# Gathering expert rows of u and v in turn, instead of four and four

## The chip, the cores and the metric

The kernel runs on one core of one Trainium2 chip. The metric is the device time of one execution in microseconds (us); the kernel before has a median of 3765.66 us over three runs, from 3763.17 to 3771.36 us.

## The reference, cut to what matters

The model is one layer of a decoder: attention with a latent cache beside a short convolution, and then a channel mixer (PEER) that looks up experts. It is computed for 1024 prompt rows and 8 sample rows, all in float32. The part that the change touches is the mixer:

```python
def peer_block(x, w_query, sub_keys, expert_u, expert_v):
    ...
    experts = jnp.take_along_axis(cidx, pos, axis=-1)      # 8 heads x 16 picks = 128 per row
    g = jax.nn.softmax(top_s, axis=-1)
    u = expert_u[experts]
    v = expert_v[experts]
    a = jax.nn.gelu(jnp.einsum('td,thkd->thk', x, u).astype(jnp.float32), approximate=False)
    return jnp.einsum('thk,thkd->td', (g * a).astype(x.dtype), v)
```

So each of the 1024 rows picks 128 experts. Of each it needs one row of u (1024 floats) for a dot product, and one row of v (1024 floats), which is added to the result with a weight made from that dot product.

## The kernel before, in words

The prompt is cut into 8 tiles of 128 rows. A tile has two halves of work. The front (`stages_of`, L80) is everything up to the choice of the experts: norm, projections, four attention heads, output projection, eight query projections with their top-16 searches, and `select`. The other half is the experts' part. The loops of all engines run it for tile `it` beside the front of tile `it + 1`; beside the eighth tile runs the front of the sample rows, which reads pages of the cache.

The experts' part of a tile has 128 slots. A slot is one gather of u and one of v, each 128 partitions by 1024 floats, 524,288 bytes. Slots go in groups of G = 4, so a tile has 32 groups, g = 0 to 31 (the trace's L numbers are lines of the kernel before). `u_ring` and `v_ring` hold RING = 8 slots each, two groups.

What each engine does for group g of a tile, in the order of its own queue:

- DVE (L1339 and on): the four dot products of group g + 1 (`dot_group`, L1301; each waits for its own u gather), then the weights of group g (`weigh_group`, L1307), then its part of the front stages that `beside(g, T)` puts there, about one stage a group.
- ACT: the gelu of group g + 1 (L918, waits for all four dot products), then four diagonal matrices of group g from its weights (L925), then its front stages.
- PE: its part of the front stages, then `v_group` of group g (L676): 16 matrix products of `v_ring` with the diagonals, in two pairs of slots. A pair's two slots of `v_ring` are told free with the last products of the pair.
- POOL: it only issues gathers (L1438), all from one queue and in order. It waits for `u_free` of a slot (the dot product made 8 slots earlier) or `v_free` (the matrix products made 8 slots earlier), then issues. At the start of a tile it waits for the picks.
- SP: it loads the weights of the front in pieces of 1 MB, from its own DMA queue.

The order of POOL's queue is written out by hand in `tile` (L1454) and `gather_group` (L1441). There the loop over g is:

```python
for g in range(GROUPS):
    if g + 1 < GROUPS:
        gather_group(it, g + 1, "expert_u", u_ring, u_loaded)
    gather_group(it, g, "expert_v", v_ring, v_loaded)
```

Of the kernel before, what the change touches and what calls it, by code (L numbers as in the profile page):

```python
# [45 lines left out]
SLOTS = PH * TOPK  # L46
# [17 lines left out]
G = 4  # L64
GROUPS = SLOTS // G
RING = 2 * G
# [63 lines left out]
def build(nc, a, out):  # L130

    with ExitStack() as ctx:
        def sb(name, shape, dt=F32):
            return ctx.enter_context(nc.sbuf_tensor(name, shape, dt))

        on = namedtuple("Events", EVENTS)(*[ctx.enter_context(nc.semaphore(n)) for n in EVENTS])
        w_loaded = [ctx.enter_context(nc.semaphore(f"w_loaded{r}")) for r in range(WR)]
        u_loaded = [ctx.enter_context(nc.semaphore(f"u_loaded{r}")) for r in range(RING)]
        v_loaded = [ctx.enter_context(nc.semaphore(f"v_loaded{r}")) for r in range(RING)]
# [24 lines left out]
        u_ring = sb("u_ring", [P, RING, D])  # L164
        v_ring = sb("v_ring", [P, RING, D])
        ident2 = sb("ident2", [P, HB])
        diag = sb("diag", [P, RING, HB])
        pick_cur = sb("pick_cur", [P, SLOTS], U32)
# [90 lines left out]
        def waited(eng):  # L259


            eng.nop(nofuse=True)
# [1168 lines left out]
        @block.gpsimd  # L1431
        def _(pool):
            pool.memset(ckv_rows[:], 0.0).then_inc(on.zeroed, 1)
            pool.memset(ckvT[:], 0.0).then_inc(on.zeroed, 1)
            pool.memset(krT[:], 0.0).then_inc(on.zeroed, 1)

            def gather(table, ring, slot, loaded, pick):
                pool.indirect_dma_start(ring[:, slot, :], None, a[table][0],  # L1438
                                        bass.IndirectOffsetOnAxis(ap=pick, axis=0)).then_inc(loaded[slot], 16)

            def gather_group(it, g, table, ring, loaded):  # L1441
                if g * G == SLOTS // 2:

                    pool.wait_ge(on.picks_moved, it + 1)
                for s in range(g * G, (g + 1) * G):

                    if table == "expert_u":
                        pool.wait_ge(on.u_free, it * SLOTS + s + 1)
                    else:
                        pool.wait_ge(on.v_free, it * SLOTS + s + 1)  # L1450
                    waited(pool)
                    gather(table, ring, s % RING, loaded, pick_cur[:, s:s + 1])

            def tile(it):  # L1454

                pool.wait_ge(on.picked_moved, it + 1)
                gather_group(it, 0, "expert_u", u_ring, u_loaded)
                for g in range(GROUPS):
                    if g + 1 < GROUPS:
                        gather_group(it, g + 1, "expert_u", u_ring, u_loaded)  # L1460
                    gather_group(it, g, "expert_v", v_ring, v_loaded)

            with pool.Fori(0, LAST) as it:
                tile(it)
            tile(LAST)

            pool.wait_ge(on.s_slots, 1)
            pool.wait_ge(on.u_free, TILES * SLOTS + RING)
            for t in range(SB):
                gather("expert_u", u_ring, t, u_loaded, s_pick[:, t:t + 1])  # L1470
            pool.wait_ge(on.v_free, RING + TILES * SLOTS)
            for t in range(SB):
                gather("expert_v", v_ring, t, v_loaded, s_pick[:, t:t + 1])
# [55 lines left out]
```

## Time and profile before

| | |
|---|---|
| median of three runs | 3765.66 us |
| the profiled execution's own time | 3763.41 us |
| its span, first to last instruction | 3761.6 us |
| busy: PE, DVE, POOL, ACT | 2722.4, 2312.8, 2320.3, 839.3 us |
| mean granted TensorE clock | 0.858 |
| DMA over the span | 1320.97 MB, 351 GB/s |
| gathers of u and v | 1024 and 1024 (and 8 and 8 for the sample rows) |
| issue to landing, median, u and v | 11.8 and 10.5 us |

Times of rows are us from the first instruction. "Idle before" is the time for which an engine had nothing to do before an instruction, and the releaser is what ended it. A gather's busy time on POOL is the making of its descriptors; its transfer goes on behind it on the DMA engines. Tile it = 3 of the experts' part lies at about 1500 to 1900 us, it = 4 begins at about 1900, and the eighth tile lies beside the sample rows from about 3140 on.

### The profile page before, as it was taken

The numbers are of one execution on the slowest core, as the hardware profiler recorded it, in microseconds if no ns is written. First come the engines' busy times: TensorE is split into PE (matmuls) and PEld (weight loads), VectorE is DVE, ScalarE is ACT, GpSimd is POOL, SyncE is SP. The second block draws the span as 40 slices with busy tenths as digits, with TensorE's granted clock in tenths as the row PEclk, the third lists the DMA queues.
The fourth block names the chain that finished last, engine by engine and source line by source line (L and its number), as shares of the span: only waits on it lengthen the run. The fifth ranks groups of instructions, "written<-read, shape, count | busy, mean of one in ns | idle before, by whom it ended". The sixth has DMA issues, their size and how long they took to land.

```text
span 3761.6 us, 47573 instructions
## 1 busy us (share of the span) xinstructions
PE 2722.4 (72%) x13704; PEld 1530.3 (41%) x13704; DVE 2312.8 (61%) x5392; ACT 839.3 (22%) x2103; POOL 2320.3 (62%) x2071
## 2 busy tenths in 40 slices
PE   7738875687657865797568765886578766999874
PEld 5525442444324532444235432443244434533351
DVE  2384668565865578466865577566846586344474
ACT  1111311222122312232132212231123212122211
POOL 0027776766767676667666676677676776555542
PEclk9868987898879987898779887998789987899976
DMA  5149999999999999999999999999999999989884
GB/s 181 67 162 412 371 398 389 372 397 349 411 348 412 365 402 367 400 374 390 409 352 411 360 408 352 411 366 403 368 388 377 396 407 360 344 295 308 290 311 163
DMA packets 371469, 1320.97 MB, mean 351 GB/s; under 512 B 59397, under 2 KB 78383, under 8 KB 348137
## 3 DMA queue, kind: packets, MB, share of 16 engines
q0 software_dynamic: 297216, 1082.26, 75.1%
q1 hardware_dynamic: 70436, 229.74, 15.8%
q10 hardware_dynamic: 3524, 5.57, 0.4%
q8 instruction: 123, 2.02, 0.2%
q14 instruction: 170, 1.38, 0.1%
HBM read 1311.80 MB, written 5.62 MB: 350 GB/s over the span
## 4 chain that ended last, share of the span: by engine, by line
PE 34%; DVE 31%; DMA 14%; issue 12%; ACT 5%; POOL 2%; SPq 1%; DVEq 1%; ACTq 0%; POOLq 0%
DVE u_ring L1301 11%; PE acc L676 10%; DMA v_ring<-in_expert_v,pick_cur 7%; PE front L405 6%; DMA u_ring<-in_expert_u,pick_cur 4%; PE front L512 3%; PE front L533 3%; PE front L561 2%; ACT diag L925 2%; DVE sv L1192 2%; PE front L513 2%; DMA w_ring<-in_w_pieces 2%; DVE si_u L1193 2%; PE front L636 2%; DVE work L1192 1%
## 5 line engine op out<-in xcount | busy, mean ns | idle before, releaser
L1438 POOL DMA_INDIRECT v_ring<-in_expert_v,pick_cur x1024 | 1195.5, 1167 | 723.6 <-PE acc L676 460.8
L676 PE MATMUL acc<-v_ring,diag 128*64 128x512 f32 x4096 | 1172.0, 719 | 599.7 <-ACT diag L925 437.6
L1438 POOL DMA_INDIRECT u_ring<-in_expert_u,pick_cur x1024 | 1105.0, 1079 | 652.6 <-issue 289.5
L1301 DVE CUSTOM_DVE_ANT_0 u_ring<-u_ring,xn_cur 128x1024 f32<-128x1024 f32 x1024 | 1211.2, 1223 | 270.7 <-DMA u_ring<-in_expert_u,pick_cur 256.2
L676 PEld LDWEIGHTS acc<-v_ring,diag 128*64 128x64 f32 x4096 | 343.7, 162 | 1268.9 <-issue 693.4
L405 PE MATMUL front<-work,w_ring 128*128 128x128 f32 (+1 forms) x4896 | 603.5, 282 | 6.7 <-DVE work L1185 5.3
L405 PEld LDWEIGHTS front<-work,w_ring 128*128 128x128 f32 x4896 | 589.4, 200 | 41.8 <-issue 33.1
L918 ACT ACTIVATE gelu<-dots 128x4 f32<-128x4 f32 x256 | 52.6, 206 | 1835.5 <-DVE dots L1301 1834.6
L925 ACT ACTIVATE diag<-ident,wgt 128x64 f32<-128x64 f32 x1024 | 271.5, 336 | 121.6 <-DVE wgt L1307 119.9
L561 PE MATMUL front<-w_ring,work 128*128 128x256 f32 (+1 forms) x576 | 148.8, 424 | 76.5 <-DVE work L1160 66.9
L561 PEld LDWEIGHTS front<-w_ring,work 128*128 128x128 f32 (+1 forms) x576 | 116.0, 204 | 113.5 <-issue 62.7
L1192 DVE MAX8 sv<-work 128x8 f32<-128x128 f32 (+1 forms) x288 | 83.1, 288 | 120.6 <-ACT work L907 104.0
L533 PE MATMUL front<-work,ckv_rows 128*128 128x128 f32 x1024 | 133.5, 293 | 23.2 <-ACT work L871 23.2
L533 PEld LDWEIGHTS front<-work,ckv_rows 128*128 128x128 f32 x1024 | 127.6, 206 | 43.0 <-issue 42.0
L512 PE MATMUL front<-ckvT,rows_next 128*128 128x512 f32 x256 | 125.1, 611 | 1.2 <-ACT rows_next L866 1.2
L412 PE MATMUL front<-ident,work 128*128 128x128 f32 (+1 forms) x72 | 16.8, 408 | 145.2 <-DVE work L1015 145.2
L1121 DVE COPY rows_next<-front 128x512 f32<-128x512 f32 x32 | 22.1, 691 | 154.4 <-PE front L618 154.4
L918 ACT ACT_TABLE_LOAD x83 | 106.5, 1283 | 1.5
L1093 DVE SCALAR_TENSOR_TENSOR work<-low_keys,small,front 128x512 f32<-128x512 f32 x64 | 45.0, 744 | 99.3 <-PE front L513 99.3
L1169 DVE TENSOR_TENSOR rows_next<-front,x_t 128x512 f32<-128x512 f32 (+1 forms) x18 | 11.6, 684 | 123.5 <-PE front L561 123.5
L1301 DVE DVE_READ_ACCUMULATOR2_ANT dots<- 128x1 f32 x1024 | 82.3, 80 | 0.0
L1193 DVE FIND_INDEX8 si_u<-sv,work 128x8 uint32<-128x128 f32 (+1 forms) x288 | 81.7, 284 | 0.3 <-issue 0.3
(241 smaller groups left out, 2394.9 us busy)
## 6 DMA issues: line engine op xcount, KB each, us to landing
w_ring<-in_w_pieces SPq DMA_DIRECT2D x180, 1024.0 KB, 8.6
u_ring<-in_expert_u,pick_cur POOLq DMA_INDIRECT x1024, 11.8
v_ring<-in_expert_v,pick_cur POOLq DMA_INDIRECT x1024, 10.5
work<-in_cache_ckv SPq DMA_DIRECT2D x64, 128.0 KB
w_ring<-in_w_pieces SPq DMA_DIRECT2D x9, 768.0 KB, 7.4
x_t<-in_x_prompt SPq DMA_DIRECT2D x8, 512.0 KB
out_y_prompt<-work ACTq DMA_DIRECT2D x8, 512.0 KB
ckv_rows<-in_cache_ckv SPq DMA_DIRECT2D x32, 128.0 KB
```

The costliest lines, as they stand in the source:

```text
L405: last = nc.tensor.matmul(dst, w[:, k, c0:c0 + m], xT[:, k * T:(k + 1) * T], start=(k == 0), stop=(k == DC - 1))
L512: nc.tensor.matmul(F[half][:, :], q_lat[:, c, h, :], ckvT[:, c, ks], start=(c == 0), stop=False)
L513: last = nc.tensor.matmul(F[half][:, :], q_ro[:, h, :], krT[:, ks], start=False, stop=True)
L533: last = nc.tensor.matmul(F[4][:, c * P:(c + 1) * P], ckv_rows[:, j, c * P:(c + 1) * P], W[1][:, j * P:(j + 1) * P], start=(j == 0), stop= ...
L561: last = nc.tensor.matmul(dst, W[2][:, k * T:(k + 1) * T], w[:, k, :], start=(k == 0), stop=(k == DC - 1))
L676: last = nc.tensor.matmul(acc[rows, half, :], diag[:, s % RING, :], v_ring[:, s % RING, half * 512:half * 512 + 512], start=False, stop=(s ...
L918: nc.scalar.activation(gelu[:, g * G:(g + 1) * G], dots[:, g * G:(g + 1) * G], ACT.Gelu).then_inc(on.gelu_done, 1)
L925: nc.scalar.activation(diag[:, s % RING, :], ident2[:], ACT.Copy, scale=wgt[:, s:s + 1]).then_inc(on.diag_made, 1)
L1192: own(v.max(best, scores), held=True)
L1193: last = v.max_index(index[:, 8 * r:8 * r + 8], best, scores)
L1301: v.tensor_tensor_reduce(u_ring[:, slot, :], u_ring[:, slot, :], xn2_cur[:, block_of(r), :], 1.0, 0.0, ALU.mult, ALU.add, dots[:, g * G + ...
L1438: pool.indirect_dma_start(ring[:, slot, :], None, a[table][0], bass.IndirectOffsetOnAxis(ap=pick, axis=0)).then_inc(loaded[slot], 16)
```

## The change: the order in which POOL issues

Before, POOL issues the four u gathers of group g + 1 and then the four v gathers of group g. After, it issues the first four u gathers of a tile, and then for every slot s one u gather (slot s + 4) and one v gather (slot s). The last four slots have a v gather alone, as before. The wait for the second half of the picks stands ahead of the u gather of slot 64, as before. Each gather waits for the same semaphore value as before, lands in the same slot and is counted on the same semaphore. No other engine's program is changed.

```diff
--- before.py
+++ after.py
@@ -1438,27 +1438,27 @@
                 pool.indirect_dma_start(ring[:, slot, :], None, a[table][0],
                                         bass.IndirectOffsetOnAxis(ap=pick, axis=0)).then_inc(loaded[slot], 16)
 
-            def gather_group(it, g, table, ring, loaded):
-                if g * G == SLOTS // 2:
-
-                    pool.wait_ge(on.picks_moved, it + 1)
-                for s in range(g * G, (g + 1) * G):
-
-                    if table == "expert_u":
-                        pool.wait_ge(on.u_free, it * SLOTS + s + 1)
-                    else:
-                        pool.wait_ge(on.v_free, it * SLOTS + s + 1)
-                    waited(pool)
-                    gather(table, ring, s % RING, loaded, pick_cur[:, s:s + 1])
+            def gather_u(it, s):
+                pool.wait_ge(on.u_free, it * SLOTS + s + 1)
+                waited(pool)
+                gather("expert_u", u_ring, s % RING, u_loaded, pick_cur[:, s:s + 1])
+
+            def gather_v(it, s):
+                pool.wait_ge(on.v_free, it * SLOTS + s + 1)
+                waited(pool)
+                gather("expert_v", v_ring, s % RING, v_loaded, pick_cur[:, s:s + 1])
 
             def tile(it):
 
                 pool.wait_ge(on.picked_moved, it + 1)
-                gather_group(it, 0, "expert_u", u_ring, u_loaded)
-                for g in range(GROUPS):
-                    if g + 1 < GROUPS:
-                        gather_group(it, g + 1, "expert_u", u_ring, u_loaded)
-                    gather_group(it, g, "expert_v", v_ring, v_loaded)
+                for s in range(G):
+                    gather_u(it, s)
+                for s in range(SLOTS):
+                    if s + G == SLOTS // 2:
+                        pool.wait_ge(on.picks_moved, it + 1)
+                    if s + G < SLOTS:
+                        gather_u(it, s + G)
+                    gather_v(it, s)
 
             with pool.Fori(0, LAST) as it:
                 tile(it)
```

## Rows read from the trace of the kernel before

**Rows 1.** The page, its head and part 1: the whole span.

```profile
span 3761.6 us, 47573 instructions
...
PE 2722.4 (72%) x13704; PEld 1530.3 (41%) x13704; DVE 2312.8 (61%) x5392; ACT 839.3 (22%) x2103; POOL 2320.3 (62%) x2071
```

**Rows 2.** The page, part 5: costliest groups (busy, mean ns, idle before, releaser).

```profile
L1438 POOL DMA_INDIRECT v_ring<-in_expert_v,pick_cur x1024 | 1195.5, 1167 | 723.6 <-PE acc L676 460.8
...
L1438 POOL DMA_INDIRECT u_ring<-in_expert_u,pick_cur x1024 | 1105.0, 1079 | 652.6 <-issue 289.5
L1301 DVE CUSTOM_DVE_ANT_0 u_ring<-u_ring,xn_cur 128x1024 f32<-128x1024 f32 x1024 | 1211.2, 1223 | 270.7 <-DMA u_ring<-in_expert_u,pick_cur 256.2
```

**Rows 3.** Windows: us, busy (count) of five engines, PEclk, DMA share, GB/s.

```profile
1532.00:1658.00 126.00, 105.00 (x567) 60.10 (x567) 73.75 (x138) 34.81 (x84) 84.42 (x80) 0.92 1.02 411
1658.00:1706.00 48.00, 37.11 (x184) 19.61 (x180) 29.82 (x51) 16.62 (x35) 35.07 (x29) 0.93 0.90 312
...
1718.00:1730.00 12.00, 10.52 (x47) 6.49 (x46) 3.38 (x5) 0.00 (x0) 3.22 (x4) 1.00 1.02 421
1730.00:1880.00 150.00, 96.22 (x488) 51.15 (x488) 117.58 (x332) 23.04 (x81) 108.47 (x99) 0.83 1.02 409
1880.00:1903.00 23.00, 11.66 (x34) 3.62 (x36) 21.70 (x43) 6.31 (x17) 11.35 (x10) 0.62 0.76 266
1903.00:1952.00 49.00, 29.62 (x172) 18.90 (x168) 25.68 (x57) 15.55 (x33) 31.73 (x31) 0.83 0.96 365
...
3200.00:3690.00 490.00, 431.61 (x2041) 206.86 (x2040) 244.57 (x631) 109.32 (x268) 251.37 (x213) 0.88 0.86 299
```

**Rows 4.** Waits, whole span: engine, line, releaser: total us, times, longest.

```profile
POOL v_ring L1438 <- PE acc L676: 460.8, 185, 23.3
...
DVE u_ring L1301 <- DMA u_ring<-in_expert_u,pick_cur: 256.2, 97, 8.2
...
PE acc L676 <- DMA v_ring<-in_expert_v,pick_cur: 161.7, 77, 9.5
...
POOL u_ring L1438 <- DVE dots L1301: 93.7, 34, 5.6
```

**Rows 5.** Timeline of POOL, 1936 to 1960: start, us, gather, idle before.

```profile
1937.20 0.94 POOL L1438 DMA_INDIRECT u_ring<-in_expert_u,pick_cur  x1 [0.30 <-issue]
...
1940.93 0.94 POOL L1438 DMA_INDIRECT u_ring<-in_expert_u,pick_cur  x1 [0.30 <-issue]
1946.80 1.25 POOL L1438 DMA_INDIRECT v_ring<-in_expert_v,pick_cur  x1 [4.93 <-PE acc L676]
...
1951.88 0.93 POOL L1438 DMA_INDIRECT v_ring<-in_expert_v,pick_cur  x1 [0.30 <-issue]
```

**Rows 6.** Timeline of POOL, 1715 to 1731.

```profile
1719.95 0.94 POOL L1438 DMA_INDIRECT u_ring<-in_expert_u,pick_cur  x1 [0.31 <-issue]
1729.05 0.94 POOL L1438 DMA_INDIRECT v_ring<-in_expert_v,pick_cur  x1 [8.16 <-PE acc L676]
```

**Rows 7.** Timeline of DVE, 1594 to 1624.

```profile
1618.70 1.23 DVE L1301 CUSTOM_DVE_ANT_0 u_ring<-u_ring,xn_cur 128x1024 f32<-128x1024 f32 x1 [3.23 <-DMA u_ring<-in_expert_u,pick_cur]
```

**Rows 8.** Timeline of DVE, 1794 to 1802.

```profile
1796.89 1.23 DVE L1301 CUSTOM_DVE_ANT_0 u_ring<-u_ring,xn_cur 128x1024 f32<-128x1024 f32 x1 [0.17 <-DVE work L1193]
```

**Rows 9.** Timeline of POOL, 1684 to 1700.

```profile
1686.32 0.93 POOL L1438 DMA_INDIRECT v_ring<-in_expert_v,pick_cur  x1 [0.30 <-issue]
...
1691.99 1.98 POOL L1438 DMA_INDIRECT v_ring<-in_expert_v,pick_cur  x1 [0.30 <-issue]
```

**Rows 10.** Waits of POOL, 3200 to 3690.

```profile
POOL v_ring L1438 <- PE acc L676: 110.3, 27, 23.3
POOL u_ring L1438 <- DVE dots L1301: 64.3, 18, 5.6
```

**Rows 11.** Tile u_ring, whole span: duration ns least, median, most.

```profile
L1438 POOL DMA_INDIRECT u_ring<-in_expert_u,pick_cur x1024: 933/937/4547, 255.8 to 3644.9; - x171
```

## The prediction

> **What bounds the kernel now.** I read the totals first. No engine is full: PE is busy for 72% of the span, POOL for 62%, DVE for 61% [rows 1]. Then the windows, for what the DMA engines move. In the long stretches 1532 to 1658 and 1730 to 1880 they move 411 and 409 GB/s at a DMA share above 1, in three others less: 312 GB/s in 1658 to 1706 (the attention heads of the next tile stand beside the gathers there), 266 in 1880 to 1903 (`select` on DVE), 365 in 1903 to 1952 (the change of tile and the first front stages) [rows 3]. So the seven prompt tiles are bound by the DMA engines, but for two stretches a tile in which the chain of front stages and experts' groups through DVE, ACT and PE is slower than the gathers. A gather is 524,288 bytes, at 410 GB/s 1.28 us. POOL's own pace is hardly faster: 0.94 us of work and 0.30 between, 1.24 us [rows 5]. It can't make good what the DMA engines miss.
>
> In a prompt tile, time is bytes over 410 GB/s plus the time in which the DMA engines have too little to do, and this is set by how far POOL runs ahead. The waits show what stops it: 460.8 us for v slots that PE had not freed, 93.7 us for u slots that DVE had not freed [rows 4]. The timeline of one such wait shows the order at work: four u gathers go out from 1937.20 to 1940.93, POOL then stands for 4.93 us until PE frees a v slot at about 1946.8, and the four v gathers follow [rows 5]. The u gathers ahead of the wait are what the DMA engines work on meanwhile.
>
> **What the change moves.** No gather is added or removed; POOL's 2048 issues keep their cost (1167 and 1079 ns on average [rows 2]) and no other queue is touched. SP's weight pieces go their own way. Number the places of POOL's queue from P for group g. Before, u of group g + 1 has P + 1 to P + 4 and v of group g has P + 5 to P + 8. After, they are P + 1, 3, 5, 7 and P + 2, 4, 6, 8. Two things follow.
>
> First, the last u gather is 3 places later. DVE makes the dot products of group g + 1 ahead of the weights of group g and of its front stages, and ACT's gelu of g + 1 stands ahead of the diagonals of g. So the whole chain, and PE's v products of group g with it, starts a group up to 3 x 1.28 = 3.8 us later, wherever it waits for gathers. v being there sooner doesn't help, since its products wait for the diagonals.
>
> Second, POOL meets a full v ring at P + 2, not P + 5. Three u gathers that were in flight during the wait stand behind it; they are put out after it, at most 3.8 us of DMA work moved out of the wait.
>
> While the DMA engines are full, neither costs anything at once: 16 slots are in flight or waiting. Each costs where the bound changes hands. At an entry into a chain-bound stretch the chain starts later; at an exit the DMA engines have three gathers less behind them. For tile it = 3 to 4:
>
> - Entry to the heads. The last group for which DVE waits for a u gather begins at 1618.70, after 3.23 us of waiting [rows 7], so the shift shows whole: 3.8 us.
> - End of the heads. The four v gathers go out from 1686.32 to 1691.99, 5.7 us [rows 9]. With u gathers between, the last is six issues behind the first, 6 x 1.24 = 7.4 us, and one of two slow issues more, 0.5: 7.9, so 2.2 us.
> - Behind the heads. POOL waits 8.16 us with its last u gather out at 1719.95 [rows 6]. The window 1718 to 1730 still has 421 GB/s [rows 3], from the u gathers and weight pieces together. Three gathers less leave 3.8 us of it empty.
> - Entry to the query stages. From 1796.89 DVE no longer waits for gathers (the 0.17 us ahead is its own work [rows 8]); it is busy 117.58 of 150 us there [rows 3]. Some 1 us of slack may take part of the shift: 2.8 us.
> - Change of tile. The wait of 4.93 us [rows 5] with 365 GB/s around it: 3.8 us.
>
> That is 16.4 us a tile, and 7 x 16.4 = 115 us. The eighth tile I cost at nothing: 299 GB/s in 3200 to 3690 [rows 3], POOL waits 110.3 us there for PE and 64.3 for DVE [rows 10], and the gathers are not what the others wait for. That cover is the whole ring; were it gone, its 32 groups at most 3.8 us each, 122 us.
>
> The waits themselves can't be seen in the trace before in their new place, so both ends. Above: five places paid twice, once in each of the two ways, 5 x 7.7 x 7 = 270 us. Below: the v gathers of a group start 3 places sooner, and should PE be waiting for just them, 3.8 us a tile for each of two exits come back, 7 x 7.7 = 54 us faster. I take 115, nearer to the middle of the upper side, as three of the five places rest on a wait that stands in a row. The profiled execution took 3763.4 us, so 3878; the median is 2.3 us above it, so 3880 us.
>
> **A rule weighed.** POOL's gather takes 937 ns in the median, 1079 on average [rows 2, 11]; over both tables the excess is 1024 x (0.230 + 0.142) = 381 us. The Trainium skill (SBUF — State Buffer, section "SBUF: two separate sides") says that descriptors of a DMA issued from GpSimd can't be written while DVE holds the port pair that they share. That would let the order matter in another way, by what stands beside DVE's dot products. By that rule alone the sum would be the third rival's; by the rows the dot products stay as many and as long (1223 ns [rows 2]), and I add nothing.
>
> **The rivals.**
>
> 1. No change. The u gathers held back aren't needed, as DVE reaches them late anyway, and the chain has slack where I put an entry. For it: DVE waits for u gathers only 256.2 us in all [rows 4]. Against it: 312 GB/s means DMA time that never comes back. 3766 us, from 3758 to 3773.
> 2. Faster: the wait that ends last is PE's for v. PE waits 161.7 us for v gathers, 77 times [rows 4], and POOL's queue keeps v behind four u gathers, which may themselves wait for DVE (93.7 us [rows 4], 64.3 of it in the eighth tile [rows 10]). With v in turn, two exits a tile give back 7.7 us: 3766 - 54 = 3712 us. It decides if the diagonals are ready before v at the exits. Against it: DVE and ACT work for the diagonals needs the last u, which comes later.
> 3. Faster: POOL's slow issues become fewer, as dot products spread out when u gathers land two places apart. It counts only where DMA isn't full, 48 + 23 + 49 of about 410 us a tile [rows 3], 29% of 381 us; half of it 55 us: 3711 us.
> 4. Slower by more: the short waits of the query stages (1730 to 1880, DVE and DMA both nearly full [rows 3]) each start to cost. 270 us: 4036 us.
>
> That the order doesn't change as told can't be: POOL's queue is in order.
>
> **How the numbers follow.** Forecast 0.66 (3795 to 3940: from exits alone, 54 us and less, to 175 us), smaller loss 0.08 (3773 to 3795), no change 0.10, rival 2 0.09, rival 3 0.03, rival 4 0.04. A difference under 0.2%, 7.5 us, can't be told from none. Faster 0.12, same 0.10, slower 0.78. The range reaches from 3770 to 3940 and leaves out the faster cases, the top and part of no change, some 2 in 10. The forecast's own range is 3795 to 3940.
>
> **What would show it.** The DMA mean falls from 351 to about 341 GB/s (the same 1321 MB). The heads' window falls below 312 GB/s and gets longer. DVE waits for u gathers more than 256.2 us, with new waits right behind POOL's long ones. Every long wait of POOL for PE has one u gather in front since the last v, not four. The eighth tile, from the first sample stage to the end, keeps its length within 10 us. I am wrong if the DVE wait for u grows and the span doesn't, if the eighth tile takes the loss, or if PE's wait for v gathers falls by some 50 us and the span with it.

## The result, and the profile after

The changed kernel takes 3964.57 us in the median of four runs (3956.39 to 3970.27), the kernel before 3764.41 (3756.78 to 3771.36). The ratio is 1.0522, 95% interval 1.0500 to 1.0545: 200 us slower. In a later batch, beside other experiments, it was 3969.59 against 3772.97, ratio 1.0526 (1.0509 to 1.0544). Every median here is of fast executions; left out are one of experiment 5 (11936 us), four of experiment 11 (4010 to 4024 us) and two of the kernel before beside experiments 17 and 18 (3952 and 3961 us). I had forecast slower by 115 us. The direction holds, the size does not: 3965 us lies above the range of 3770 to 3940.

The head of the page and parts 1 and 2 of the changed kernel, to be set against [rows 1]:

```profile
span 3968.4 us, 47573 instructions
...
PE 2778.9 (70%) x13704; PEld 1559.0 (39%) x13704; DVE 2316.7 (58%) x5392; ACT 838.0 (21%) x2103; POOL 2329.6 (59%) x2071
...
DMA  4249999999989999999989998999989999888894
GB/s 172 83 170 400 339 379 349 351 363 339 404 312 387 346 391 348 356 350 368 395 316 388 333 395 325 395 330 379 368 332 368 351 399 346 314 296 295 283 344 154
```

DVE, ACT and POOL are busy for as long as before (DVE 2316.7 against 2312.8 us), spread over 207 us more. PE is busy 57 us longer, at a mean granted clock of 0.840 instead of 0.858. The DMA engines move the same 1321 MB, and the mean is 333 instead of 351 GB/s. The costliest groups of the changed kernel (busy, mean ns, idle before, releaser), to be set against [rows 2]:

```profile
L1438 POOL DMA_INDIRECT v_ring<-in_expert_v,pick_cur x1024 | 1158.4, 1131 | 991.3 <-PE acc L676 573.4
...
L1301 DVE CUSTOM_DVE_ANT_0 u_ring<-u_ring,xn_cur 128x1024 f32<-128x1024 f32 x1024 | 1216.2, 1223 | 565.5 <-DMA u_ring<-in_expert_u,pick_cur 553.9
L1438 POOL DMA_INDIRECT u_ring<-in_expert_u,pick_cur x1024 | 1151.4, 1124 | 582.7 <-issue 279.7
```

A gather of v is 36 ns cheaper to issue and one of u 45 ns dearer: the sum of the two is 2255 ns against 2246. So the issues themselves cost nothing, and POOL's work isn't where the time went. DVE's idle time ahead of the dot products has doubled, 270.7 to 565.5 us. The waits name what it waits for (total us, times, longest; against [rows 4]):

```profile
PE acc L676 <- ACT diag L925: 741.4, 150, 10.8
...
POOL v_ring L1438 <- PE acc L676: 573.4, 147, 19.5
DVE u_ring L1301 <- DMA u_ring<-in_expert_u,pick_cur: 553.9, 280, 7.7
...
POOL v_ring L1438 <- DVE dots L1301: 134.5, 31, 22.8
```

DVE's wait for u gathers rises from 256.2 us in 97 waits to 553.9 in 280. It is now more often a wait of one or two us ahead of a single dot product where there was one long wait ahead of four. POOL's wait for PE rises as well; how much of it costs something by itself these rows can't say. PE's wait for diagonals was, before:

```profile
PE acc L676 <- ACT diag L925: 437.6, 97, 10.8
```

PE's wait for v gathers, 161.7 us before [rows 4], has no line left in the full list of the changed kernel's waits. And the gathers land sooner behind their issue (last column of part 6: 11.8 and 10.5 us before):

```profile
u_ring<-in_expert_u,pick_cur POOLq DMA_INDIRECT x1024, 7.5
v_ring<-in_expert_v,pick_cur POOLq DMA_INDIRECT x1024, 7.3
```

So fewer gathers stand in front of each at the DMA engines. By stretch of a tile (columns as in [rows 3]; tile it = 4, which begins at 2008 us here; the last line is the sample rows' tile):

```profile
2010.00:2065.00 55.00, 28.57 (x172) 18.73 (x168) 24.21 (x50) 14.20 (x27) 34.16 (x31) 0.80 0.86 319
2187.00:2235.00 48.00, 37.46 (x178) 20.87 (x176) 26.82 (x48) 13.12 (x32) 33.42 (x30) 0.89 0.89 312
2275.00:2315.00 40.00, 24.96 (x129) 13.95 (x130) 19.78 (x53) 4.39 (x18) 30.16 (x27) 0.83 0.99 387
2315.00:2436.00 121.00, 71.86 (x354) 37.60 (x352) 100.78 (x284) 17.11 (x61) 82.23 (x72) 0.83 0.98 376
3390.00:3890.00 500.00, 438.54 (x2066) 213.32 (x2064) 241.23 (x608) 109.07 (x270) 248.30 (x219) 0.88 0.83 299
```

The first line is most of groups 0 to 3, the second the heads, the third groups 19 to 21, the fourth most of the query stages, groups 22 to 31. The same groups of tile it = 4 before, for the second to the fourth line:

```profile
2067.00:2115.00 48.00, 37.95 (x190) 19.96 (x186) 29.93 (x51) 17.61 (x35) 34.41 (x29) 0.94 0.91 326
2148.00:2181.00 33.00, 23.25 (x124) 12.87 (x124) 21.96 (x56) 4.53 (x18) 26.29 (x23) 0.90 0.98 383
2181.00:2302.00 121.00, 73.77 (x366) 38.45 (x364) 100.75 (x284) 17.12 (x61) 83.84 (x75) 0.82 0.99 394
```

The heads move 312 GB/s against 326; in tile it = 3 the same 48 us move 319 against 312 [rows 3], so nothing stands out there, and my sign of a fall in the heads' window did not come. The query stages move 376 against 394 in the same time: there the DMA engines have less left to do. To place the loss I take, for each tile, the start of the first dot product of a group (L1301 on DVE's timeline) and the mean over tiles it = 1 to 6, in us a tile:

| kernel | groups 0-3 | 4-11 | 12-15 | 16, 17 | 18-21 | 22-31 | tile |
|---|---|---|---|---|---|---|---|
| before | 56.5 | 96.0 | 47.5 | 36.8 | 43.0 | 131.2 | 410.9 |
| changed | +8.2 | +5.2 | +1.2 | +4.1 | +8.1 | -0.3 | +26.5 |

The tile it = 0 loses 28 us, six tiles 26.5 each (159), the sample rows' tile 18 (9 in the repetition), and the first dot product begins 2 us later: 207 us, the difference of the spans.

Where the time shows is not always where the DMA engines missed work. Counted from the DMA records over the same six tiles, groups 12 and 13 take 28.2 us in both kernels but move 7.9 MB instead of 10.6, and groups 20 and 21 take 33.7 us instead of 26.1, move 13.2 MB instead of 10.1, and do so at 393 GB/s against 387. There the engines make good what they missed ahead of it. In groups 0 to 3 they fall from 369 to 325 GB/s on the spot.

What happens in the first column is seen on DVE. The dot products of groups 1, 2 and 3 of tile 4 in the changed kernel (start, length, idle time before and releaser):

```profile
2016.57 1.23 DVE L1301 CUSTOM_DVE_ANT_0 u_ring<-u_ring,xn_cur 128x1024 f32<-128x1024 f32 x1
2017.72 0.08 DVE L1301 DVE_READ_ACCUMULATOR2_ANT dots<- 128x1 f32 x1
...
2020.38 1.22 DVE L1301 CUSTOM_DVE_ANT_0 u_ring<-u_ring,xn_cur 128x1024 f32<-128x1024 f32 x1 [1.43 <-DMA u_ring<-in_expert_u,pick_cur]
...
2023.55 1.23 DVE L1301 CUSTOM_DVE_ANT_0 u_ring<-u_ring,xn_cur 128x1024 f32<-128x1024 f32 x1 [1.94 <-DMA u_ring<-in_expert_u,pick_cur]
...
2039.42 1.21 DVE L1301 CUSTOM_DVE_ANT_0 u_ring<-u_ring,xn_cur 128x1024 f32<-128x1024 f32 x1
...
2055.37 1.22 DVE L1301 CUSTOM_DVE_ANT_0 u_ring<-u_ring,xn_cur 128x1024 f32<-128x1024 f32 x1
2056.51 0.08 DVE L1301 DVE_READ_ACCUMULATOR2_ANT dots<- 128x1 f32 x1
...
2058.67 1.23 DVE L1301 CUSTOM_DVE_ANT_0 u_ring<-u_ring,xn_cur 128x1024 f32<-128x1024 f32 x1 [0.93 <-DMA u_ring<-in_expert_u,pick_cur]
...
2064.05 1.23 DVE L1301 CUSTOM_DVE_ANT_0 u_ring<-u_ring,xn_cur 128x1024 f32<-128x1024 f32 x1 [4.15 <-DMA u_ring<-in_expert_u,pick_cur]
```

The four dot products of a group take 4.7 us if their rows are there. In group 1 they take 8.2 us, from 2016.57 to 2024.8, and in group 3, from 2055.37, 9.9 us; in the same tile before the change both took 4.7, group 3 from 1946.02 to 1950.7:

```profile
1946.02 1.22 DVE L1301 CUSTOM_DVE_ANT_0 u_ring<-u_ring,xn_cur 128x1024 f32<-128x1024 f32 x1
...
1949.45 1.22 DVE L1301 CUSTOM_DVE_ANT_0 u_ring<-u_ring,xn_cur 128x1024 f32<-128x1024 f32 x1
```

In the mean of the six tiles group 1 takes 8.1 us and group 3 takes 9.0, each 4.7 before: 7.7 of the 8.2 us of the column. DVE's queue is in order, and the front stage that stands behind the dot products waits with them. POOL's side of group 3 (columns as in [rows 5]):

```profile
2031.46 1.72 POOL L1438 DMA_INDIRECT u_ring<-in_expert_u,pick_cur  x1 [0.30 <-issue]
2041.70 0.93 POOL L1438 DMA_INDIRECT v_ring<-in_expert_v,pick_cur  x1 [8.52 <-PE acc L676]
2042.93 1.97 POOL L1438 DMA_INDIRECT u_ring<-in_expert_u,pick_cur  x1 [0.30 <-PE acc L676]
...
2046.45 0.94 POOL L1438 DMA_INDIRECT u_ring<-in_expert_u,pick_cur  x1 [0.30 <-issue]
...
2048.94 0.93 POOL L1438 DMA_INDIRECT u_ring<-in_expert_u,pick_cur  x1 [0.30 <-issue]
```

POOL waits 8.52 us for a v slot with one u gather in front, as expected, where four had been out in [rows 5]. The other three then go out at 2042.93, 2046.45 and 2048.94, and the last of them has its dot product only at 2064.05, 15 us behind its issue (it landed just before; why it took twice the median no row shows). So in group 3 it is the u gathers held behind POOL's wait that DVE meets on their way; in group 1 POOL doesn't wait, and the four go out 2.5 to 4.2 us apart with v gathers between them.

### The profile page after: what moved, and what is told of

It reads as the page before. It is cut to its first block, busy times and chain, and to the rows that moved or that the text cites. A ratio compares the mean times of both kernels' runs of the same rounds, so it can differ in the third digit from the quotient of the medians.

```text
span 3968.4 us, 47573 instructions
## 1 busy us (share of the span) xinstructions
PE 2778.9 (70%) x13704; PEld 1559.0 (39%) x13704; DVE 2316.7 (58%) x5392; ACT 838.0 (21%) x2103; POOL 2329.6 (59%) x2071
## 4 chain that ended last, share of the span: by engine, by line
DVE 28%; PE 28%; DMA 16%; issue 16%; POOL 5%; ACT 5%; SPq 2%; DVEq 1%; POOLq 0%; ACTq 0%
DMA u_ring<-in_expert_u,pick_cur 13%; DVE u_ring L1301 9%; PE acc L676 8%; PE front L405 3%; PE front L512 3%; PE front L561 3%; POOL v_ring L1438 3%; PE front L533 2%; POOL u_ring L1438 2%; ACT diag L925 2%; DVE sv L1192 2%; DVE si_u L1193 2%; PE front L513 2%; DVE work L1192 2%; PE front L636 1%
## 5 line engine op out<-in xcount | busy, mean ns | idle before, releaser
L1438 POOL DMA_INDIRECT v_ring<-in_expert_v,pick_cur x1024 | 1158.4, 1131 | 991.3 <-PE acc L676 573.4
L676 PE MATMUL acc<-v_ring,diag 128*64 128x512 f32 x4096 | 1214.1, 747 | 741.6 <-ACT diag L925 741.4
L1301 DVE CUSTOM_DVE_ANT_0 u_ring<-u_ring,xn_cur 128x1024 f32<-128x1024 f32 x1024 | 1216.2, 1223 | 565.5 <-DMA u_ring<-in_expert_u,pick_cur 553.9
L1438 POOL DMA_INDIRECT u_ring<-in_expert_u,pick_cur x1024 | 1151.4, 1124 | 582.7 <-issue 279.7
L676 PEld LDWEIGHTS acc<-v_ring,diag 128*64 128x64 f32 x4096 | 362.8, 171 | 1442.0 <-ACT diag L925 796.3
L412 PEld LDWEIGHTS front<-ident,work 128*128 128x128 f32 (+1 forms) x72 | 13.5, 222 | 183.3 <-DVE work L1015 183.3
L1301 DVE DVE_READ_ACCUMULATOR2_ANT dots<- 128x1 f32 x1024 | 82.7, 81 | 0.0
```

The source lines that it names most:

```text
L676: last = nc.tensor.matmul(acc[rows, half, :], diag[:, s % RING, :], v_ring[:, s % RING, half * 512:half * 512 + 512], start=False, stop=(s ...
L1301: v.tensor_tensor_reduce(u_ring[:, slot, :], u_ring[:, slot, :], xn2_cur[:, block_of(r), :], 1.0, 0.0, ALU.mult, ALU.add, dots[:, g * G + ...
```

## The experiments

"u" and "v" in an order are the four u gathers of group g + 1 and the four v gathers of group g, from left to right. In brackets stands the 95% interval of the ratio to the kernel before in the same batch.

**1. v's first gather early.** Order u v u u u v v v.

```diff
-                for s in range(SLOTS):
-                    ...
-                    gather_v(it, s)
+                for g in range(GROUPS):
+                    for table, r in [('u',0),('v',0),('u',1),('u',2),('u',3),('v',1),('v',2),('v',3)]:
+                        s = (g + 1) * G + r if table == "u" else g * G + r
+                        ...
```

> Order of a group's eight places: u, v, u, u, u, v, v, v (u of group g + 1, v of group g), so only the first v gather comes ahead of its old place. The last u gather is 1 place later than in the kernel before (3 in the changed kernel), and 3 u gathers stand behind the first v gather's wait (3 in the changed kernel). Theory A (all of the 200 us comes from the last u gather, by its places): before + 67 us, 3831. Theory B (all comes from the u gathers held behind the wait for a v slot): before + 200, 3964. Both in equal parts, as my sum had it: before + 133, 3897. Rival C (issuing the two tables in turn costs by itself, by the number of changes of table): 4 changes a group against 8 and 2, before + 67.

3872.34 us against 3766.54 for the kernel before beside experiments 1 to 4, ratio 1.0283 (1.0241 to 1.0324), + 106. DVE's waits (columns as above):

```profile
DVE u_ring L1301 <- DMA u_ring<-in_expert_u,pick_cur: 415.7, 187, 8.3
```

**2. u's last gather late.** The same edit with the order u u u v v v u v.

> Order of a group's eight places: u, u, u, v, v, v, u, v. The last u gather is 3 places later, as in the changed kernel, but only 1 u gather stands behind the first v gather's wait. Theory A (the last u gather's place): before + 200 us, 3964. Theory B (gathers held behind the wait): before + 67, 3831. Both in equal parts: 3897. Rival C (changes of table): before + 67. Rival D (the last v gather comes further behind the first, 4 issues against 3 before and 6 in the changed kernel): before + 67.

3895.35 us, ratio 1.0345 (1.0306 to 1.0384), + 129.

```profile
DVE u_ring L1301 <- DMA u_ring<-in_expert_u,pick_cur: 479.0, 156, 10.2
```

Neither theory A nor B gives both numbers. Against the changed kernel, the first has the same three u gathers held behind the v wait, the last of them two places sooner and the third one place: 92 us less. The second has the same last place and two fewer held: 69 us less. So both matter.

**3. In turn, with u seven slots ahead.**

```diff
-                for s in range(G):
+                for s in range(7):
                     gather_u(it, s)
                 for s in range(SLOTS):
-                    if s + G == SLOTS // 2:
+                    if s + 7 == SLOTS // 2:
                         pool.wait_ge(on.picks_moved, it + 1)
-                    if s + G < SLOTS:
-                        gather_u(it, s + G)
+                    if s + 7 < SLOTS:
+                        gather_u(it, s + 7)
                     gather_v(it, s)
```

> u and v strictly in turn, as in the changed kernel, but with u seven slots ahead of v instead of four: u gather of slot s + 7, then v gather of slot s. All four u gathers of group g + 1 are then out before the first v gather of group g, as before, and u is never fewer than seven slots ahead. Theories A and B (what matters is how far ahead u stands, not the turns): the 200 us are gone, 3764 within 20, perhaps 10 to 20 us faster than before, as u stands further ahead than before at the end of a group. Rival C (the turns themselves): 3964. Rival D (the four v gathers of a group spread over seven issues): 3964 as well, since the spread is that of the changed kernel. Rival E (a u gather seven slots ahead waits for a dot product and holds the v gathers behind it): slower than before by tens of us, with POOL's waits for DVE above 200 us.

3816.48 us, ratio 1.0128 (1.0085 to 1.0171), + 50.

```profile
PE acc L676 <- DMA v_ring<-in_expert_v,pick_cur: 318.1, 118, 8.2
...
POOL u_ring L1438 <- DVE dots L1301: 228.6, 76, 8.0
DVE u_ring L1301 <- DMA u_ring<-in_expert_u,pick_cur: 208.4, 132, 5.5
```

This is as strictly in turn as the changed kernel, and three quarters of the loss are gone: taking turns by itself costs 50 us at most (rival C, which had all 200 in it, is out), and the spread of the v gathers (D) is at most the rest. In the means of six tiles the dot products of groups 1, 3, 15, 16 and 20 take 4.7 to 5.1 us again, where the changed kernel takes 8.1, 9.0, 11.7, 9.4 and 10.5. The rest fits rival E: POOL's wait for dot products rises from 93.7 [rows 4] to 228.6 us, and the v gathers behind it come late (PE's wait for them 318.1 against 161.7 us). Some 28 us of the 50 are in the prompt tiles and 23 in the sample rows' tile, where five single groups are 3 to 8 us longer.

**4. In turn, with u five slots ahead.** The same edit with 5 for 7.

> u and v strictly in turn with u five slots ahead of v. The last u gather of group g + 1 stands 1 place later than before, and 2 u gathers stand behind the first v gather's wait. Theory A: before + 67, 3831. Theory B: before + 133, 3897. Both in equal parts: 3864. Rivals C and D (turns, spread of v): 3964, no different from four slots ahead.

3867.42 us, ratio 1.0264 (1.0217 to 1.0312), + 101.

```profile
DVE u_ring L1301 <- DMA u_ring<-in_expert_u,pick_cur: 439.9, 238, 6.4
```

The expectation has a place wrong: with five slots ahead the last u gather of a group has two v gathers newly in front of it, not one. (The fourth u gather of group g + 1 goes out with the v gather of slot 4g + 2, behind those of 4g and 4g + 1.) So the first experiment has one place and three held gathers, the fourth two places and two held: 106 and 101 us. That tells neither theory from the other; two equal parts, 33 us for each place and each held gather, would give 133 for both.

**5 to 8. By which way does a late u gather cost?** Two chains hang on it: the weights, diagonals and v products of group g, and DVE's front stages, which stand behind the dot products in its queue. Experiments 5 and 6 take the weights out from behind the dot products, for four and four and for in turn; 7 and 8 take out the weights and the front stages. None takes out the front stages alone.

```diff
   DVE (5, 6)
+                    if g and T == P:
+                        weigh_group(it, g)
                     if g and g + 1 < GROUPS:
                         dot_group(it, g + 1, 0, half)
-                    if g:
+                    if g and T != P:
                         weigh_group(it, g)
   ACT (5, 6)
-                    if g and T == P and g + 1 < GROUPS:
-                        gelu_group(it, g + 1)
                     if g:
                         diag_group(it, g)
+                    if g and T == P and g + 1 < GROUPS:
+                        gelu_group(it, g + 1)
```

In 7 and 8 the four dot products of a prompt tile's group stand behind DVE's stages (`dot_group(it, g + 1, 0 if T == P else half, G)` there), and the gelu behind ACT's.

> The kernel before (four and four), with the weights of group g ahead of the four dot products of group g + 1 in DVE's queue, and the diagonals of g ahead of the gelu of g + 1 in ACT's. PE's v products of a group then no longer hang on the u gathers of the next. It is the base for the run beside it. Theory A (the chain through the u gathers sets part of the time in the kernel before too): 10 to 60 us faster than before. If the chain isn't what ends last before: 3766 within 10. Slower only if the dot products, now a little later, free u slots late.

> The changed kernel (in turn) with the same two swaps. After the first four runs: one place of the last u gather costs some 46 us, three of the 200 us' parts hang on it. Theory A by way of the weights (last u gather, dot product, gelu, weights, diagonals, v products): the difference between in turn and four and four falls from 200 us to under 80 with the swaps. Theory A by way of DVE's queue (DVE's front stages stand behind the dot products that wait for the last u gather): it stays above 150 us. Theory B (held gathers) or D (spread v gathers): stays near 200.

> The kernel before (four and four), with the dot products of group g + 1 behind DVE's front stages of group g, and the gelu of g + 1 behind ACT's front stages: neither the weights nor the front stages of a group stand behind a wait for u gathers of the next. Base for the run beside it. u slots are freed later by a stage. Either faster by 10 to 60 us (the chain was what ended last) or slower (u slots freed late: POOL's wait for DVE above 200 us).

> The changed kernel (in turn) with the same move. Theory A in either way: the difference to its base falls under 80 us (what is left is B and D). Theories B or D: 150 to 200 us. If A works through DVE's queue alone, the difference falls here and not with the weights swapped.

| | four and four | in turn | difference |
|---|---|---|---|
| as they are | 3764.41 | 3964.57 | 200 |
| weights first (5, 6) | 3713.54, ratio 0.9849 (0.9815 to 0.9882) | 3900.40, ratio 1.0351 (1.0320 to 1.0382) | 187 |
| dot products last (7, 8) | 3848.35, ratio 1.0211 (1.0176 to 1.0247) | 3919.34, ratio 1.0401 (1.0375 to 1.0428) | 71 |

The first row is of the first batch; beside 5 to 8 the kernel before took 3772.55 us. The waits of 5, then of 6:

```profile
PE acc L676 <- DMA v_ring<-in_expert_v,pick_cur: 449.0, 176, 9.5
...
DVE u_ring L1301 <- DMA u_ring<-in_expert_u,pick_cur: 316.6, 126, 9.2
...
PE acc L676 <- ACT diag L925: 69.8, 17, 8.1
```

```profile
DVE u_ring L1301 <- DMA u_ring<-in_expert_u,pick_cur: 572.3, 312, 6.3
...
PE acc L676 <- ACT diag L925: 285.9, 68, 10.8
PE acc L676 <- DMA v_ring<-in_expert_v,pick_cur: 285.5, 115, 8.2
```

and of 7, then of 8:

```profile
POOL u_ring L1438 <- DVE dots L1299: 474.3, 142, 11.2
...
DVE u_ring L1299 <- DMA u_ring<-in_expert_u,pick_cur: 33.4, 21, 4.5
```

```profile
POOL u_ring L1438 <- DVE dots L1299: 314.1, 110, 11.3
...
DVE u_ring L1299 <- DMA u_ring<-in_expert_u,pick_cur: 193.0, 105, 5.6
```

With the weights first, PE waits less for diagonals (69.8 us in 5 against 437.6 in the kernel before, 285.9 in 6 against 741.4 in the changed one), and the difference stays. DVE still waits 316.6 and 572.3 us for u gathers, with its stages behind. With the dot products behind the stages, DVE waits 33.4 and 193.0 us, and the difference falls to 71. So the loss goes through DVE's in-order queue: what stands behind the waiting dot products there. Two reservations. The kernel of 7 is itself slower (POOL waits 474.3 us for u slots that DVE frees a stage later) and may hide a part of the difference. And the front stages' own share isn't isolated: they are enough for most of the loss without the swapped weights, but in 6 PE's 285.9 us for diagonals remain, since the weights of a group still stand behind what DVE did in the group ahead.

**9 to 12. Which groups pay?** In turn for some groups of a tile only, and a fourth order, u u u v v v v u.

```diff
+                    turns = [in turn] if g >= 22 else [four and four]      # 9;  g < 12: 10;  12 <= g < 22: 11
+                    for table, r in turns:
```

> In turn only for groups 22 to 31 of a tile (the query and select stages beside them), four and four for the rest. In the trace of the changed kernel these ten groups take as long as before (130.9 against 131.2 us a tile). If that is because DVE is full there, this costs nothing beyond 2 us a tile: 3766 to 3780. My prediction had 2.8 us a tile at the entry of these stages and 3.8 at the change of tile: 3766 + 46 = 3812 if both stand. If it costs more than half of the 200 us, the loss seen in the early groups of the changed kernel is handed over from these.

> In turn only for groups 0 to 11 of a tile (input norm, projections, convolution beside them). By the changed kernel's trace these lose 13.4 us a tile: 3766 + 94 = 3860 if each part pays its own loss. Under 3800 if the loss there comes from the order in the groups ahead of them.

> In turn only for groups 12 to 21 of a tile (heads, output projection, norms beside them). By the changed kernel's trace these lose 13.4 us a tile: 3766 + 94 = 3860. With the two runs beside it the sum should come to some 200 us if the parts add up; if the three sum to much less, what costs is two parts together (an exit and the next entry).

> Order of a group's eight places: u, u, u, v, v, v, v, u. The last u gather is 4 places later than before, 1 u gather stands behind the v wait, and the four v gathers follow each other without a gap, as before. With 46 us for each place of the last u gather (changed kernel against the first experiment) it is before + 175 to 185, 3945. If the spread of the v gathers were what costs (theory D), it would be under the second experiment's 3895: 3850 or less. If each held gather were what costs, before + 67: 3833.

In this batch the kernel before itself took 3931.08 us (22 runs, 3904.77 to 3960.71), so its numbers stand only against each other: 3923.37, ratio 0.9986 (0.9942 to 1.0031); 3998.96, 1.0149 (1.0095 to 1.0204); 3973.39, 1.0093 (1.0050 to 1.0135); 3974.00, 1.0095 (1.0060 to 1.0130). In turn from group 22 on costs nothing that can be measured in this batch, in which the other orders cost less too. The others I repeated, with the changed kernel beside them.

> In turn for groups 0 to 11 alone, again, since the last job ran on a chip where the kernel before itself took 3931 us and gathers landed more slowly (there: + 68 us, 1.5%). The changed kernel runs beside it this time. If its cost here is the loss that the changed kernel's trace shows in these groups, 13.4 us a tile: half of what the changed kernel loses, + 94 of 200 where the kernel before takes 3766.

> In turn for groups 12 to 21 alone, again (on the slower chip + 58 us). By the trace 13.4 us a tile, + 94 where the changed kernel has + 200. If this and the run before it sum to the changed kernel's loss, each stretch pays for itself and groups 22 to 31 pay nothing.

> u, u, u, v, v, v, v, u, again (on the slower chip + 43 us, far less than the 180 I had expected, but there the changed kernel was not measured). With the last u gather's place alone: nine tenths of the changed kernel's loss or more, + 180. If in the second experiment (u, u, u, v, v, v, u, v: + 129) it was the place of one u gather only, this one is + 130 to 175. Under + 100 says that the number of u gathers that come late matters more than how late the last is: in the changed kernel three come late (by 1, 2 and 3 places), here one by 4.

> The changed kernel beside them, for the measure of a whole loss on the same chip. Where the kernel before takes 3766: + 200. On the slower chip, if gathers bind there more and the chain less: less than 200, some + 130 (the two parts' 68 + 58).

The kernel before: 3772.97 us. Groups 0 to 11: 3857.43, ratio 1.0223 (1.0196 to 1.0251). Groups 12 to 21: 3860.16, 1.0240 (1.0221 to 1.0258). u u u v v v v u: 3928.66, 1.0418 (1.0393 to 1.0443). The changed kernel: 3969.59, 1.0526. DVE's waits in the three:

```profile
DVE u_ring L1301 <- DMA u_ring<-in_expert_u,pick_cur: 404.6, 208, 6.5
```

```profile
DVE u_ring L1301 <- DMA u_ring<-in_expert_u,pick_cur: 373.9, 163, 8.0
```

```profile
DVE u_ring L1301 <- DMA u_ring<-in_expert_u,pick_cur: 539.8, 146, 11.8
```

84 + 87 = 171 of 197 us: the two parts are most of it, and each loses in its own groups. By the table's measure (mean over tiles it = 1 to 6), groups 0 to 11 in turn lose 7.8 and 3.9 us a tile in the first two columns and nothing behind; groups 12 to 21 lose 1.3, 3.2 and 7.5 in the next three and nothing elsewhere. One u gather four places late costs 156 us, and three places late 129 (experiment 2). The changed kernel has that one three places late and two others by one and two: they add some 70 us. Counted over all orders, the places by which a group's u gathers go out later, taken together, follow the loss best:

| order | places late, in sum | u gathers behind the first v gather | loss, us | us a place |
|---|---|---|---|---|
| u v u u u v v v | 3 | 3 | 106 | 35 |
| in turn, five ahead | 3 | 2 | 101 | 34 |
| u u u v v v u v | 3 | 1 | 129 | 43 |
| u u u v v v v u | 4 | 1 | 156 | 39 |
| in turn, four ahead | 6 | 3 | 200 | 33 |

(With five ahead, the first of the four also goes out one place earlier.) Every gather that is late in place also stands behind the first v gather and its wait, so these orders can't part the two ways.

**17, 18. A version meant to beat both.**

```diff
   DVE (18), on top of 5; ACT's gelu likewise
+                    behind = T == P and (g in (16, 17) or g >= 22)
-                    if g and g + 1 < GROUPS:
+                    if g and not behind and g + 1 < GROUPS:
                         dot_group(it, g + 1, 0, half)
                     ...
-                        dot_group(it, g + 1, half, G)
+                        dot_group(it, g + 1, 0 if behind else half, G)
```

> Four and four with the weights of a group ahead of the next group's dot products, again with more rounds, as a candidate that beats both kernels: 1.5% faster than before, 3717 where before takes 3770.

> The same, and in groups 16, 17 and 22 to 31 of a tile also the next group's dot products behind DVE's front stages and the gelu behind ACT's. By the traces of the two earlier runs the dot products last take 9.2 us less a tile in groups 16 and 17 and 5.9 less in 22 to 31 (3.0 less with the weights first alone), and lose only in groups 8 to 15 and 18 to 21, where they stay first here. If the stretches add up as the parts of the change did: 7 x (9.2 + 2.9) = 85 us faster than the run beside it, 3632. If the gain in 16 and 17 was only work handed back from the groups ahead of them (they lost 13.9 + 3.9 there), 0 to 20 us.

The kernel before took 3916.13 us this time. The fifth experiment's kernel took 3887.91, ratio 0.9917 (0.9880 to 0.9953): faster again, by half as much. With the dot products behind the stages in some groups: 3959.35, ratio 1.0119 (1.0079 to 1.0158), slower. Here the stretches did not add up:

```profile
POOL u_ring L1442 <- DVE dots L1302: 323.6, 75, 18.1
```

POOL's wait for dot products is 323.6 us (74.4 in its neighbour). That fits the expectation's second case, that the 9 us gained in groups 16 and 17 in the seventh experiment were work that the groups ahead had lost; it isn't shown by itself. The best kernel found is the fifth's.

## Why the prediction was wrong in size

**What bounds it: right.** Prompt tiles go by the DMA engines except where the chain through the engines is slower, and the loss is DMA time without work (351 to 333 GB/s; I had forecast 341). The query stages, bound by DVE, lose nothing, and the sample rows' tile little.

**The direction and the way: right in half.** I gave two ways: the last u gather three places later, and three u gathers held behind POOL's wait for v. The orders tried don't part them, and the trace has both at work: the places in group 1, the holding in group 3. Of the first, I had the whole chain start later by way of gelu, weights and diagonals, and DVE's front stages with it. With the weights taken out from behind the dot products, 187 of 200 us stay; with the front stages out as well, 71. So it is most of all DVE's own queue that starts later.

**The terms.** By groups, forecast and measured, in us a tile:

| term | forecast | measured |
|---|---|---|
| change of tile (groups 0 to 3) | 3.8 | 8.2 |
| entry to the heads (4 to 11) | 3.8 | 5.2 |
| end of the heads (12 to 15) | 2.2 | 1.2 |
| behind the heads (16 to 21) | 3.8 | 12.2 |
| entry to the query stages (22 to 31) | 2.8 | -0.3 |
| sum | 16.4 | 26.5 |

The step that failed is the price of the exits, change of tile and behind the heads: 7.6 forecast, 20.4 measured. I priced each exit once, as three gathers of 1.28 us moved out of one wait. It is paid in each group that follows in which DVE meets u gathers on their way, held or 2.5 us and more apart: four dot products then take 8 to 13 us in the mean, in groups 1, 3, 15, 16, 20 and 21, where they took 4.7 or 4.8 (7.2 in group 21). The rows had half of it: four gathers at POOL's pace of 1.24 us [rows 5] just keep up with a dot product of 1.22 us [rows 2]; every second one can't, unless, as with u seven slots ahead, it went out early enough. I followed positions in the queue and never laid DVE's group out in time. And a part of what shows behind the heads was missed by the DMA engines in groups 12 and 13 already, as the bytes above say. The entries were nearly right where a wait stood in a row [rows 7] and wrong where I only guessed at slack [rows 8].

**The eighth tile**, at nothing, cost 18 and 9 us in two profiles. My upper end, each place paid twice, was 270 us and had a chance of 4%: rival 4 with its 270 is nearest in mechanism (short waits that each cost), but not in place, since the query stages that it named lose nothing.

**The rule weighed.** Issues of u and v take 2255 ns in sum, 2246 before, so the order changed nothing there, and rival 3 falls. The Trainium skill (SBUF — State Buffer, section "SBUF: two separate sides") on DVE keeping GpSimd from writing descriptors gives the sum no term. The traces agree with it as far as they go: before, 271 of the 279 issues longer than 1.7 us overlap a dot product, of the 1579 shorter than 1.1 us only 29% do; after, 257 of 269 and 40%. Which port a dot product uses no row shows. Rival 2 falls as well, and with it my sign for it: PE's wait for v gathers went from 161.7 us to nothing, but the span rose, as PE's wait for diagonals rose instead (437.6 to 741.4 us).

**What stays open.** How much of the loss is the places and how much the holding; whether the lower granted clock (0.840 against 0.858, with PE busy 57 us longer) adds to the loss or only follows from PE's waits, which no run separates; and how much of the 50 us with u seven slots ahead is the spread of v and how much POOL's wait for dot products. I didn't try a larger v ring.

## What to carry to other kernels

In an in-order queue that feeds two consumers, ask when the whole of a group has landed for the one whose own queue has other work behind it. Here interleaving alone, with that consumer's gathers still out in time (seven slots ahead), cost 50 us; interleaving that also made them late cost 200. Price such a change by laying out the consumer's group in time at each group where it catches up with the transfers, not once per place. And take work that needs nothing new out from behind the wait: the weights of a group ahead of the next group's dot products gave 1.5% (0.8% in another batch) by two calls swapped in each of two queues.

## What the runs showed of the hardware that I had not expected

The same kernel before took 3764 to 3773 us in four batches and 3931 and 3916 us in two others, the last of them on a chip that had shown 3767 before. The clock of its runs there is hardly lower (0.843 to 0.855 against 0.851 to 0.860). The profiles of the kernels beside it that have four and four in groups 4 to 7 show slower gathers there: 392 to 406 GB/s against 413, where gathers set most of the time. Why, no run shows. There the effects were smaller in part (0.99 instead of 0.985, 1.015 instead of 1.022, 1.010 instead of 1.042), so I compare ratios of this kernel only within one batch.
